# Retention values centred by a TensorE product, their copy on ScalarE, and the NSA compression one tile later

## The chip, the cores and the metric
One NeuronCore of one Trainium2 chip runs the whole program in one launch. The time is the device time of that core in microseconds: the median of three runs, with their lowest and highest. Every run computes two layers of the model below for a sequence of 512 positions.

## What is computed
Two layers of a mixer with four branches and a gated feed-forward part, all in float32. What matters here:

```python
h = rms_norm(x, norm1_g); z = h @ w_in            # 512 x 1024 times 1024 x D_IN
# retention, for each of 4 heads of 128: zq, zk, zv, zg from z
scores = einsum(q, k) * intra                     # decay mask
o = scores @ v (+ the state from earlier chunks)
mu  = mean(o, axis=-1); var = mean((o - mu)**2)
o = (o - mu) * rsqrt(var + EPS) * gn_g * silu(zg)
# NSA branch, compression of keys and values
tb  = t[:, blk] + cmp_pe                          # windows of 32, stride 16
hid = gelu(einsum('bnlgd,lde->bnge', tb, w1)); out = hid @ w2
k_c = rotary(compress(k_cmp)); v_c = compress(v_cmp)
```

The kernel does not subtract the mean of `o`: it centres each row of `v` over the 128 features of its head beforehand, which gives the same, since `o` is linear in `v`.

## The kernel before
All activations lie transposed, features on the 128 partitions and the 512 positions along the free axis. TensorE does every projection as 24 matmuls of 128x512: each float32 weight and each float32 activation is split into a high half and a low half in the type fp32r, and three products (high by high, high by low, low by high; L1185 to L1187) are added up in one PSUM bank, for eight chunks of 128 features. Such a product of one 128-column group of weights is called a tile here. The two banks `acc[0]` and `acc[1]` alternate; VectorE empties one (`take`, L717, multiplying by the norm's factor `rstd`) while TensorE fills the other, and `acc_free` counts the tiles emptied.

The weights stream through three slots: SP's queue loads a group of 512 KB, ScalarE makes its high half `w_hi` (`ahead`, L455, for the group two ahead, as soon as TensorE has finished the group before the present one), GpSimd makes the low half `w_lo` in two operations (L433), both with semaphores `hi_ready` and `lo_ready`. These are the only operations of GpSimd. ScalarE runs its program in order, so `ahead` stands behind whatever was written ahead of it.

A layer has four stages: 12 tiles of group A (keys, values, queries, gates; the list `A_TILES`), 32 tiles of group B (retention, short convolution, pool; `B_TILES`) beside which the attention runs, then a loop that merges the branches, then output and feed-forward. The order of group A is written out by hand on each engine: on TensorE a loop over `A_TILES` with extra steps after tile 5 (`compress`, L1268: 64 small products of the windows `win_k`, `win_v` with `w1k`, `w1v`), after tile 7 (`kc` and `vc`, from `hid`) and after tile 9 (`kc_swap`), and the turns of `v_slc` and `v_win` (L1277) after tiles 5 and 7; on VectorE a straight list (L811 to L853). The windows are made by L775 in four operations each. VectorE's `rotate` (L757, L759, L761) works on keys and queries with partners that ScalarE's DMA queue has copied into `rot`.

Group B has 128 slots, four to a tile, one after each quarter of the tile's 24 matmuls. The table `SIDE` lists for each slot what is done there, and every engine walks through it and does its own part. For head h of the retention, whose tiles rq, rk, rv, rg stand at `RET0[h]` = 0, 16, 20, 24, `ret_turn` is in the last slot of tile rg (15, 79, 95, 111). `ret_scores` and `ret_values` (L1408, L1418, with VectorE's L944 between them, which multiplies by the decay mask and makes `pr`) begin at `RET_SLOT[h]` = 68, 80, 96, 112. So for heads 1 to 3 the turn is in the slot just before the first scores, and for head 0 it is far ahead. `ret_end` of heads 0 to 3 (L973, L975) stands in slots 79, 88, 104 and 122: that of head 0 in the slot of head 1's turn, ahead of it. Its reciprocals are L964 and L967.

`ret_turn` before: TensorE turns the four 128x128 blocks of `rv_T` into one PSUM bank (`turn4`, L1277); VectorE sums each row of each block (L951, to `v_sum`) and writes `rv` as the block less 1/128 of that sum (L952). `ret_values` of the head waits for it through `t_free`. The banks `t_bank` are also used by the attention's turns until slot 70; `t_free` counts their release in the order of `T_USES`.

The last stage spreads the final norm's factors over the partitions by four products with the identity (L1523). Before the first tile TensorE multiplies zeros ten times (L1180).

Of the kernel before, what the change touches and what calls it, by code (L numbers as in the profile page):

```python
# [147 lines left out]
V_MADE = ["win_k", "k0_scaled", "k1_scaled", "win_v", "k0", "k1", "arg", "hid", "q0", "q1", "q2", "q3", "kc"]  # L148
# [13 lines left out]
V_MADE.append("branches")  # L162
# [20 lines left out]
def build(nc, xT, weights, vec, w1, pool_w, consts, decay, out):  # L183
    with ExitStack() as ctx:
# [72 lines left out]
        w2v = at("w2v", [P, DH], F32, R4 + 4 * QT * 3 * HEADS + 4 * 224)  # L257
        den = small[:, 64:68]
# [185 lines left out]
        def _(act):  # L444
# [64 lines left out]
            with act.Fori(0, LAYERS) as L:  # L509

                for g in range(A_GROUPS):
                    if g:
                        ahead(L, g)
                    if g == 3:
                        root("sumsq1", L)
                    if 1 <= g <= 4:
                        act.wait_ge(acc_free, 1 + L * TILES + g)
                        nc.scalar.activation((k_cmp[:, :], v_cmp[:, :], kT[:, 0, :], kT[:, 1, :])[g - 1], acc[(g - 1) % 2][:, :],
                                             ACT.Copy).then_inc(acc_free, 1)
                    for name in ("k0", "k1", "q0", "q1", "q2", "q3"):  # L520
                        if A_AT[name] == g - 1:
                            rotate_partners(L, name)
                    if g == 6:
                        act.wait_ge(v_made, v_count(L, "arg"))
                        nc.scalar.activation(hid_a, hid_a, ACT.Tanh, scale=0.7978845608028654).then_inc(a_made, 1)
                    if g == 11:
                        act.wait_ge(acc_free, 1 + L * TILES + 12)
                        nc.scalar.activation(sc[:, 2, :], sc[:, 2, :], ACT.Tanh, scale=0.5).then_inc(a_made, 1)


                for b in range(B_GROUPS):
# [15 lines left out]
                    for n in range(4 * b, 4 * b + 4):  # L547
                        for e in SIDE[n]:
# [14 lines left out]
                            elif e[0] == "attn_hi":  # L563
# [3 lines left out]
                                                     ACT.Copy).then_inc(a_made, 1)  # L567
                            elif e[0] == "ret_hi":
# [76 lines left out]
        def _(dve):  # L645
# [64 lines left out]
            with dve.Fori(0, LAYERS) as L:  # L710
# [111 lines left out]
                gelu_arg()  # L822
                t_wait("v_slc")
                t_end(ve.tensor_copy(v_nat[:, 0, :, :], t_of("v_slc")[:, :].rearrange("p (k n) -> p k n", k=QT)), "v_slc")
                gelu()
                take(6, qT[:, 0, :])
                take(7, qT[:, 1, :])
# [3 lines left out]

                s_wait("kc")
# [9 lines left out]
                take(8, qT[:, 2, :])  # L842
                rotate("q1", qT[:, 1, :], "cos_a", "sin_a")
# [7 lines left out]
                v_end(ve.tensor_tensor(kc[:, 0:NCMP], kc[:, 0:NCMP], kc_rot[:, 0:NCMP], ALU.add), "kc")  # L851
                dve.wait_ge(halves, 1 + L * (2 * GROUPS) + 24)
# [93 lines left out]
                def ret_turn(e):  # L946


                    t_wait(e)
                    src = t_of(e)[:, :].rearrange("p (k n) -> p k n", k=QT)  # L950
                    then(ve.tensor_reduce(v_sum, src, AX.X, ALU.add))  # L951
                    t_end(ve.scalar_tensor_tensor(out=rv[:, :, :], in0=v_sum.unsqueeze(2).to_broadcast([P, QT, RD]),  # L952
                                                  scalar=-1.0 / RD, in1=src, op0=ALU.mult, op1=ALU.add), e)
# [15 lines left out]
                def ret_end(e):  # L969
# [5 lines left out]
                    v_end(ve.scalar_tensor_tensor(out=o, in0=o, scalar=0.5, in1=rg[:, :], op0=ALU.mult, op1=ALU.mult), e)  # L975
# [198 lines left out]
        def _(pe):  # L1174
# [4 lines left out]
            for _ in range(10):  # L1179
# [9 lines left out]
            with pe.Fori(0, LAYERS) as L:  # L1189
# [91 lines left out]
                for g, name in enumerate(A_TILES):  # L1281
# [9 lines left out]
                    if g == 5:  # L1291
                        compress()
                    if g == 7:
# [104 lines left out]
                def ret_turn(e):  # L1398
                    pe.wait_ge(acc_free, 1 + L * TILES + (A_GROUPS + B_TILES.index(("rv", e[1])) + 2))
                    turn4(e, rv_T[:, :])  # L1400
# [121 lines left out]
            for t in range(QT):  # L1522
                ins = mm(s_bank[1][:, t * P:(t + 1) * P], spread(rstd[:, t:t + 1], [[0, P]]), ident, start=True, stop=True)  # L1523
# [4 lines left out]
CHAIN_LAYER, CHAIN_J, CHAIN_F, CHAIN_D = 179, 4, 15, 2  # L1528
# [117 lines left out]
```

## Time and profile before

| | |
|---|---|
| median of 3 runs | 2092.7 us (2092.09 to 2094.68) |
| profiled execution, its own time | 2092.94 us |
| its span, first to last instruction | 2091.2 us |
| mean granted TensorE clock | 0.992 of full |
| TensorE busy | 2044.3 us of the span |
| VectorE, ScalarE, GpSimd busy | 58%, 33%, 44% of the span |
| largest groups on TensorE | L1185 to L1187, the projections: 771.2, 743.3 and 744.0 us for `xg` alone |

The profiled execution is one more run of the same program; its time is 1.7 us more than its span, which runs from the first to the last instruction. "Busy" is the time in which an engine had an instruction under way. The matmuls overlap, the start of one lying before the end of the last, so the time of a group is read from starts rather than from durations. What ended an idle stretch of an engine is named behind "<-". A float32 product that is not a turn leaves two matmul records, so the x counts of such lines are twice the matmuls.

### The profile page before, as it was taken

To read this page: it belongs to the slowest core of one execution; us is meant where nothing else is said; L and a number is where in the kernel's file an instruction comes from. 1 tells how busy PE (TensorE), PEld (TensorE's weight loads), DVE (VectorE), ACT (ScalarE), POOL (GpSimd) and SP (SyncE) were. 2 spreads that over 40 slices of the span, in tenths; PEclk is the share of its full clock that TensorE was granted. 3 is DMA by queue.
4 is the path that set the end of the run, shared out by engine and by line. 5 is a ranking of instruction groups with operands and counts; after the bars stand their busy time and mean duration, and the time that the engine had idled before them with its cause. 6 is when DMAs were issued, how large, how long until landed. Compare 5 with 4: busy or idle time off the path is not lost.

```text
span 2091.2 us, 31895 instructions
## 1 busy us (share of the span) xinstructions
PE 2044.3 (98%) x9764; PEld 1637.6 (78%) x9764; DVE 1216.9 (58%) x1811; ACT 682.9 (33%) x1001; POOL 917.6 (44%) x672
## 2 busy tenths in 40 slices
PE   8999999999999999999999999899999999999997
PEld 6777667888888888888877777678888888888886
DVE  7766866523226888862257677663322278888522
ACT  5255523333232322222233554232323232222222
POOL 3422223444444555545544212335444455555552
PEclk9999999999999999999999999999999999999998
DMA  5311122223222222223233112222222222232333
GB/s 208 96 62 52 62 74 93 81 100 100 93 98 99 93 97 93 100 85 119 91 120 101 51 52 65 88 86 91 98 97 96 100 91 92 99 100 92 102 107 104
DMA packets 57431, 194.88 MB, mean 93 GB/s; under 512 B 7040, under 2 KB 7552, under 8 KB 57216
## 3 DMA queue, kind: packets, MB, share of 16 engines
q1 hardware_dynamic: 52576, 186.17, 26.6%
q10 hardware_dynamic: 4768, 7.61, 1.4%
q8 instruction: 48, 0.79, 0.2%
q14 instruction: 39, 0.32, 0.1%
HBM read 186.67 MB, written 2.10 MB: 90 GB/s over the span
## 4 chain that ended last, share of the span: by engine, by line
PE 87%; DVE 8%; issue 3%; ACT 1%; ACTq 0%; DMA 0%; DVEq 0%; SPq 0%
PE acc L1185 27%; PE acc L1187 26%; PE acc L1186 26%; PE o L1385 2%; PE s L1359 2%; PE t L1367 1%; PE o L1418 1%; PE s L1408 1%; DVE pT L967 1%; DVE pT L964 1%; DVE win_k L775 0%; DVE rk L759 0%; PE s L1268 0%; DMA w_raw<-weights_dram 0%; DVE rstd L748 0%
## 5 line engine op out<-in xcount | busy, mean ns | idle before, releaser
L433 POOL TENSOR_TENSOR w_lo<-w_raw,w_hi 128x512 fp32r<-128x512 f32 x668 | 917.4, 1394 | 1148.5 <-ACT w_hi L455 1132.3
L1185 PE MATMUL acc<-xg_hi,w_hi 128*128 128x512 f32 x1904 | 771.2, 405 | 5.6 <-DVE xg_lo L697 3.0
L1187 PE MATMUL acc<-xg_hi,w_lo 128*128 128x512 f32 x1904 | 744.0, 391 | 0.0
L1186 PE MATMUL acc<-xg_lo,w_hi 128*128 128x512 f32 x1904 | 743.3, 390 | 0.0
L455 ACT ACTIVATE w_hi<-w_raw 128x1024 fp32r<-128x1024 f32 x336 | 355.3, 1057 | 822.9 <-PE acc L1187 777.7
L1185 PEld LDWEIGHTS acc<-xg_hi,w_hi 128*128 128x128 f32 x1904 | 358.4, 188 | 114.9 <-issue 29.0
L1186 PEld LDWEIGHTS acc<-xg_lo,w_hi 128*128 128x128 f32 x1904 | 358.8, 188 | 77.8 <-issue 7.3
L1187 PEld LDWEIGHTS acc<-xg_hi,w_lo 128*128 128x128 f32 x1904 | 358.4, 188 | 76.7
L1062 DVE TENSOR_TENSOR work<-acc,rstd 128x512 f32<-128x512 f32 x64 | 44.1, 689 | 256.2 <-PE acc L1187 256.2
L1186 PE MATMUL acc<-act_lo,w_hi 128*128 128x512 f32 x352 | 136.9, 389 | 0.0
L1185 PE MATMUL acc<-act_hi,w_hi 128*128 128x512 f32 x352 | 136.9, 389 | 0.0
L1187 PE MATMUL acc<-act_hi,w_lo 128*128 128x512 f32 x352 | 136.9, 389 | 0.0
L1156 DVE SCALAR_TENSOR_TENSOR x<-acc,x 128x512 f32 x16 | 11.1, 693 | 159.9 <-PE acc L1187 159.9
L1068 DVE SCALAR_TENSOR_TENSOR work<-work,acc 128x512 f32<-128x512 f32 x64 | 44.0, 687 | 103.2 <-PE acc L1187 103.2
L1185 PE MATMUL acc<-y_hi,w_hi 128*128 128x512 f32 x256 | 99.6, 389 | 0.0
L1186 PE MATMUL acc<-y_lo,w_hi 128*128 128x512 f32 x256 | 99.6, 389 | 0.0
L1187 PE MATMUL acc<-y_hi,w_lo 128*128 128x512 f32 x256 | 99.6, 389 | 0.0
L620 ACT ACTIVATE work<-work 128x512 f32<-128x512 f32 x44 | 27.8, 632 | 189.3 <-DVE work L1111 189.3
L919 DVE COPY pT<-t 128x128 f32<-128x128 f32 (+3 forms) x128 | 56.6, 483 | 54.8 <-PE o L1385 54.7
L1187 PEld LDWEIGHTS acc<-act_hi,w_lo 128*128 128x128 f32 x352 | 66.1, 188 | 13.8
L1186 PEld LDWEIGHTS acc<-act_lo,w_hi 128*128 128x128 f32 x352 | 66.1, 188 | 13.7
L1185 PEld LDWEIGHTS acc<-act_hi,w_hi 128*128 128x128 f32 x352 | 66.1, 188 | 13.6
(207 smaller groups left out, 2237.4 us busy)
## 6 DMA issues: line engine op xcount, KB each, us to landing
w_raw<-weights_dram SPq DMA_DIRECT2D x339, 512.0 KB, 3.3
x<-xT_dram SPq DMA_DIRECT2D x8, 256.0 KB, 6.4
rot<-rq ACTq DMA_DIRECT2D x16, 128.0 KB
rot<-rk ACTq DMA_DIRECT2D x16, 128.0 KB
dec<-decay_dram ACTq DMA_DIRECT2D x8, 256.0 KB, 3.2
out_dram<-x SPq DMA_DIRECT2D x8, 256.0 KB, 2.7
con<-consts_dram SPq DMA_DIRECT2D x1, 1406.0 KB, 11.1
w1k<-w_dram SPq DMA_DIRECT2D x2, 512.0 KB, 8.8
```

The source lines that it names most:

```text
L433: nc.gpsimd.tensor_tensor(w_lo[:, slot, part], w_raw[:, slot, part], w_hi[:, slot, part].bitcast(F32), ALU.subtract).then_inc(lo_ready, 1)
L455: nc.scalar.activation(w_hi[:, slot, :], w_raw[:, slot, :], ACT.Copy).then_inc(hi_ready, 1)
L620: nc.scalar.activation(work[:, 2, :], work[:, 1, :], ACT.Tanh, scale=0.5).then_inc(silu_ready, 1)
L919: t_end(ve.tensor_copy(pT[:, u % 2, 0:w], t_of(e)[:, 0:w]), e)
L964: then(ve.reciprocal(pT[:, 1, 0:S // 2], pT[:, 1, 0:S // 2]))
L1062: ve.tensor_tensor(work[:, n, :], acc[n % 2][:, :], rstd[:, :], ALU.mult).then_inc(acc_free, 1)
L1068: ve.scalar_tensor_tensor(out=work[:, n, :], in0=work[:, n, :], scalar=1.0, in1=acc[n % 2][:, :], op0=ALU.add, op1=ALU.mult).then_inc(acc_ ...
L1185: mm(tile, w_h, right_hi, start=first, stop=False)
L1186: mm(tile, w_h, right_lo, start=False, stop=False)
L1187: return mm(tile, w_l, right_hi, start=False, stop=last)
L1359: mm(b[:, 0:w], qT[r, h % 4, qi * P:(qi + 1) * P], kT[r, br, 0:w], start=True, stop=True).then_inc(s_done, 1)
L1385: ins = mm(o_bank[qi % 2][d, j * P:(j + 1) * P], v[:, d], p[:, half, :], start=(br == 0 and k == 0), stop=(br == 1 and k == qi + 1))
```

## The change
- `ret_turn` on TensorE is four matmuls of the blocks of `rv_T` with the matrix `center` = identity - 1/128, in place of four turns, so the centred values come out of PSUM ready. VectorE's sum and subtraction go; for head 0 VectorE copies the bank to `rv`, for heads 1 to 3 ScalarE does, in its walk through `SIDE`, and counts `t_free`.
- `center` (128x128, float32) is made on VectorE once a layer, as the last thing after `kc`.
- `compress` on TensorE moves from after tile 5 to after tile 6, the products of `hid` from after tile 7 to after tile 8. On VectorE `gelu_arg` moves behind take(6), `gelu` behind take(7), and the evictions of `kc` and `vc` behind take(8) and the rotation of `q1`. On ScalarE the tanh of `hid` moves from step 6 to step 7, behind the DMAs for `q0`.
- `ret_end` waits for its own last operation.
- The zero products at the start are 14 instead of 10, and the four products of the last stage become turns.

```diff
-V_MADE = [..., "q3", "kc"]
+V_MADE = [..., "q3", "kc", "center"]
...
+        center = at("center", [P, P], F32, R4 + 4 * QT * 3 * HEADS + 4 * 224 + 4 * DH)
...
 (ScalarE, group A)
-                    if g == 6:
+                    if g == 7:
                         act.wait_ge(v_made, v_count(L, "arg"))
                         nc.scalar.activation(hid_a, hid_a, ACT.Tanh, ...)
 (ScalarE, SIDE)
+                            elif e[0] == "ret_turn" and e[1]:
+                                act.wait_ge(t_done, t_use(L, e))
+                                nc.scalar.activation(rv[:, :, :], t_of(e)[:, :].rearrange("p (k n) -> p k n", k=QT), ACT.Copy).then_inc(t_free, 1)
...
 (VectorE, group A)
                 take(5, sc[:, 1, :])
-                gelu_arg()
                 t_wait("v_slc")
                 t_end(ve.tensor_copy(v_nat[:, 0, :, :], ...), "v_slc")
+                take(6, qT[:, 0, :])
+                gelu_arg()
+                take(7, qT[:, 1, :])
                 gelu()
-                take(6, qT[:, 0, :])
-                take(7, qT[:, 1, :])
                 t_wait("v_win")
                 t_end(ve.tensor_copy(v_nat[:, 1, :, :], ...), "v_win")
                 rotate("q0", qT[:, 0, :], "cos_a", "sin_a")
+                take(8, qT[:, 2, :])
+                rotate("q1", qT[:, 1, :], "cos_a", "sin_a")
                 s_wait("kc")
                 ...
                 s_end(ins, "vc")
-                take(8, qT[:, 2, :])
-                rotate("q1", qT[:, 1, :], "cos_a", "sin_a")
                 take(9, qT[:, 3, :])
...
                 v_end(ve.tensor_tensor(kc[:, 0:NCMP], kc[:, 0:NCMP], kc_rot[:, 0:NCMP], ALU.add), "kc")
+                v_end(ve.scalar_tensor_tensor(out=center[:, :], in0=ones, scalar=-1.0 / RD, in1=ident, op0=ALU.mult, op1=ALU.add), "center")
...
 (VectorE, SIDE)
                 def ret_turn(e):
+                    if e[1]:
+                        made["t"] += 1
+                        return
                     t_wait(e)
-                    src = t_of(e)[:, :].rearrange("p (k n) -> p k n", k=QT)
-                    then(ve.tensor_reduce(v_sum, src, AX.X, ALU.add))
-                    t_end(ve.scalar_tensor_tensor(out=rv[:, :, :], in0=v_sum.unsqueeze(2).to_broadcast([P, QT, RD]),
-                                                  scalar=-1.0 / RD, in1=src, op0=ALU.mult, op1=ALU.add), e)
+                    t_end(ve.tensor_copy(rv[:, :, :], t_of(e)[:, :].rearrange("p (k n) -> p k n", k=QT)), e)
...
-                    v_end(ve.scalar_tensor_tensor(out=o, in0=o, scalar=0.5, in1=rg[:, :], ...), e)
+                    v_end(ve.scalar_tensor_tensor(out=o, in0=o, scalar=0.5, in1=rg[:, :], ...), e, wait=True)
...
 (TensorE)
-            for _ in range(10):
+            for _ in range(14):
                 mm(acc[1][:, 0:P], rstd[:, 0:P], rstd[:, 0:P], start=True, stop=True)
...
-                    if g == 5:
+                    if g == 6:
                         compress()
-                    if g == 7:
+                    if g == 8:
                         pe.wait_ge(v_made, v_count(L, "hid"))
...
                 def ret_turn(e):
                     pe.wait_ge(acc_free, ...)
-                    turn4(e, rv_T[:, :])
+                    if e[1] == 0:
+                        pe.wait_ge(v_made, v_count(L, "center"))
+                    b = t_begin(e)
+                    last_wait()
+                    for k in range(QT):
+                        ins = mm(b[:, k * P:(k + 1) * P], rv_T[:, k * P:(k + 1) * P], center[:, :], start=True, stop=True)
+                    ins.then_inc(t_done, 1)
...
             for t in range(QT):
-                ins = mm(s_bank[1][:, t * P:(t + 1) * P], spread(rstd[:, t:t + 1], [[0, P]]), ident, start=True, stop=True)
+                ins = nc.tensor.transpose(s_bank[1][:, t * P:(t + 1) * P], spread(rstd[:, t:t + 1], [[0, P]]), ident)
...
-CHAIN_LAYER, CHAIN_J, CHAIN_F, CHAIN_D = 179, 4, 15, 2
+CHAIN_LAYER, CHAIN_J, CHAIN_F, CHAIN_D = 175, 4, 15, 2
```

## Rows read from the trace of the kernel before

**Rows 1.** The page's busy times: busy us (share of the span) xinstructions.
```profile
PE 2044.3 (98%) x9764; PEld 1637.6 (78%) x9764; DVE 1216.9 (58%) x1811; ACT 682.9 (33%) x1001; POOL 917.6 (44%) x672
```

**Rows 2.** TensorE's waits: line waited for: us in total, times, longest.
```profile
PE o L1418 <- DVE pr L944: 12.6, 8, 3.9
PE s L1268 <- DVE win_v L775: 7.0, 2, 3.5
...
PE s L1408 <- DVE rk L761: 3.4, 4, 1.4
```

**Rows 3.** TensorE's timeline, tiles 5 to 7 of layer 0: start, duration, what.
```profile
49.09 0.28 PE L1268 MATMUL s<-win_k,w1k 128*64 128x62 f32 x1 [3.49 <-DVE win_v L775]
...
52.88 0.94 PE L1277 MATMUL t<-con,sc 128*128 128x128 f32 x4
53.58 0.47 PE L1185 MATMUL acc<-xg_hi,w_hi 128*128 128x512 f32 x1
...
59.15 0.39 PE L1185 MATMUL acc<-xg_hi,w_hi 128*128 128x512 f32 x1
```

**Rows 4.** Timelines of ScalarE, GpSimd and TensorE, head 1, layer 0.
```profile
281.75 1.06 ACT L455 ACTIVATE w_hi<-w_raw 128x1024 fp32r<-128x1024 f32 x1 [4.21 <-PE acc L1187]
...
282.89 2.99 POOL L433 TENSOR_TENSOR w_lo<-w_raw,w_hi 128x512 fp32r<-128x512 f32 x2 [2.74 <-ACT w_hi L455]
...
289.66 2.05 PE L1418 MATMUL o<-pr,rv 128*128 128x512 f32 x2 [3.88 <-DVE pr L944]
```

**Rows 5.** Busy time by window: PE, PEld, DVE, ACT, POOL, granted clock, DMA, GB/s.
```profile
289.66:300.10 10.44, 10.44 (x30) 7.22 (x31) 2.47 (x5) 1.06 (x1) 0.70 (x1) 0.70 0.01 2
1322.31:1331.38 9.07, 9.07 (x30) 6.57 (x31) 2.47 (x5) 1.06 (x1) 0.69 (x1) 0.81 0.01 2
```

**Rows 6.** Timelines of VectorE and TensorE, head 2, layer 0.
```profile
318.48 1.78 DVE L761 TENSOR_TENSOR rk<-rk,rot 128x512 f32<-128x512 f32 x1
...
320.49 1.10 PE L1408 MATMUL s<-rq,rk 128*128 128x512 f32 x2 [1.41 <-DVE rk L761]
...
323.50 1.10 PE L1418 MATMUL o<-pr,rv 128*128 128x512 f32 x2 [0.52 <-DVE pr L944]
```

**Rows 7.** TensorE's timeline, head 3, layer 0.
```profile
353.26 1.10 PE L1418 MATMUL o<-pr,rv 128*128 128x512 f32 x2 [0.50 <-DVE pr L944]
```

**Rows 8.** VectorE's timeline, take(4) and the last add before take(5), layer 0.
```profile
45.00 0.69 DVE L717 TENSOR_TENSOR sc<-acc,rstd 128x512 f32<-128x512 f32 x1
...
54.43 0.69 DVE L761 TENSOR_TENSOR kT<-kT,rot 128x512 f32<-128x512 f32 x1
```

**Rows 9.** VectorE's `kc` and TensorE's product of the compressed keys, layer 0.
```profile
87.32 1.26 DVE L851 TENSOR_TENSOR kc<-kc,kc_rot 128x31 f32<-128x31 f32 x1
...
89.61 1.09 PE L1339 MATMUL s<-qT,kc 64*32 64x512 f32 x16
```

**Rows 10.** TensorE's timeline: the zero products at the start; the turns of head 2.
```profile
1.71 4.40 PE L1180 MATMUL acc<-rstd 128*128 128x128 f32 x20 [1.71 <-DVE rstd L683]
...
317.10 0.60 PE L1277 MATMUL t<-con,rv_T 128*128 128x128 f32 x4
```

**Rows 11.** VectorE, head 1, layer 0; last, durations of L973 over all heads, min/median/max.
```profile
282.97 1.77 DVE L973 SCALAR_TENSOR_TENSOR pT<-pT,vec 128x512 f32<-128x512 f32 x1
284.77 1.67 DVE L975 SCALAR_TENSOR_TENSOR pT<-pT,rg 128x512 f32<-128x512 f32 x1
286.36 0.68 DVE L951 TENSOR_REDUCE small<-t 128x4 f32<-128x512 f32 x1
...
L973 DVE SCALAR_TENSOR_TENSOR pT<-pT,vec x8: 750/753/1767, 283.0 to 1403.6; 128x512 f32<-128x512 f32 x8
```

**Rows 12.** TensorE's timeline, the end of the program.
```profile
2078.06 1.87 PE L1519 MATMUL s<-con,ssq 128*128 128x1 f32 x8 [2.41 <-DVE ssq L1084]
2080.50 2.08 PE L1523 MATMUL s<-con,rstd 128*128 128x128 f32 x8 [0.57 <-DVE rstd L1166]
```

**Rows 13.** TensorE's timeline, the first matmul of tile 2, layer 0.
```profile
22.69 0.47 PE L1185 MATMUL acc<-xg_hi,w_hi 128*128 128x512 f32 x1 [0.80 <-ACT k_cmp L518]
```

More of the change, by code:

```diff
@@ L146 @@
 assert len(S_USES) % 2 == 0 and len(T_USES) % 2 == 0
-V_MADE = ["win_k", "k0_scaled", "k1_scaled", "win_v", "k0", "k1", "arg", "hid", "q0", "q1", "q2", "q3", "kc"]
+V_MADE = ["win_k", "k0_scaled", "k1_scaled", "win_v", "k0", "k1", "arg", "hid", "q0", "q1", "q2", "q3", "kc", "center"]
 A_MADE = ["hid", "gate"]
@@ L161 @@
             V_MADE.append(_e[1])
-V_MADE.append("branches")
+V_MADE += ["branches"]
 PV_MADE = [_x for _e in SEQUENCE for _x in ([_e, ("values", _e[1] + 1)] if _e[0] == "values" else [_e] if _e[0] == "ret_values" else [])]
@@ L974, in ret_end @@
                                                  op0=ALU.mult, op1=ALU.mult))
-                    v_end(ve.scalar_tensor_tensor(out=o, in0=o, scalar=0.5, in1=rg[:, :], op0=ALU.mult, op1=ALU.mult), e)
+                    v_end(ve.scalar_tensor_tensor(out=o, in0=o, scalar=0.5, in1=rg[:, :], op0=ALU.mult, op1=ALU.mult), e, wait=True)
                 def ret_split(e):
```

## The prediction
> **What bounds the kernel now.** The busy times first: TensorE is busy 98% of the span [rows 1], so only TensorE's instructions and its idle time count. The list of its waits comes next: three of them belong to stages that this diff touches, 7.0, 12.6 and 3.4 us in both layers together [rows 2]. The timelines then show the place of each. (a) After tile 5 it stands 3.49 us for VectorE's `win_v` before compressing [rows 3], and again in layer 1 [rows 2]. (b) In head 1 of the retention it stands 3.88 us for `pr` and then runs at a granted clock below full: 0.70 over 10.44 us, 0.81 over 9.07 us in layer 1 [rows 4, 5]; 0.5 of full is the lower of its two levels (1.2 of 2.4 GHz). (c) Heads 2 and 3 show waits of 1.41, 0.52 and 0.50 us [rows 6, 7]; the totals [rows 2] leave about 0.3 for the fourth (3.4 / 2 - 1.41). The sum is made against the profiled execution, 2092.94 us; the median of the runs is 0.24 us less.
>
> **Compression one tile back.** TensorE leaves tile 5 at 49.09 - 3.49 = 45.6. The turn of `v_slc` waits for take(4), done at 45.69 [rows 8], costs about 0.4, so tile 6 starts at 46.2 and lasts 59.15 - 53.58 = 5.57 [rows 3]: 51.8. The compression takes 52.88 - 49.09 = 3.8 [rows 3]: 55.6. Tile 7 also needs its accumulator emptied by take(5), behind the rotation of `k1`. Its last add starts at 54.43 and takes 0.69 [rows 8], the take another 0.6: 55.8 at best. But ScalarE's next high half starts when tile 6 ends, now 51.8, so GpSimd's next low half (from 53.8, when its present one is through, to 56.4) falls on that add, and an add between SBUF tiles beside GpSimd takes 1.78 instead of 0.69 [rows 6]. I take 56.8, a new wait of 1.2. Tile 7 started at 59.15, so 2.35 us are gained, 2.3 in layer 1: **-4.65**. Bounds: -6.6 without that collision, -2.6 if a second operation collides. `hid` moves with tiles 7 and 8 and has a tile (5.6 us) of time. `kc` now comes after the rotation of `q1`, some 5 us into tile 9 (take 0.69, three operations of 0.69, 1.78 and 1.78, `kc` itself 0.2 [rows 6, 8]), whose end asks for it at 6.1 us (5.57 and the small products): no wait, slack 1.1. ScalarE's DMAs for the rotations keep their order and follow the takes; its tanh stands behind the four for `q0` instead of before them, ready 5 us before it is needed. SP's and GpSimd's queues are passed by nothing.
>
> **`center`.** One VectorE operation of 128 columns a layer, behind `kc`. Free it would take some 0.3 us. The operation before it has 31 columns and takes 1.26 us [rows 9], which only waiting for GpSimd explains; GpSimd then has one more half to do. So I take 1.3 us, until 89.9; the gate copy behind it must free its bank (0.3 us more, with the hand-over 90.4) before L1339, now at 89.61 [rows 9]. **+1.5** for two layers; bounds 0 (it slips in) and +2.6.
>
> **Product in place of turn.** A turn of four blocks is four records, 0.60 us with the drain of the last [rows 10]. A plain product leaves two records (L1408 is one matmul, "x2" [rows 6]). At the low level 20 records took 4.40 us, 0.22 each [rows 10], so about 0.11 at full clock. Four more records of 0.11 to 0.13 make +0.5 us a head. In head 0 nothing covers it: **+1.0** for two layers. In head 1 it falls into the wait. Bounds a head: 0.44, and 1.35 if a plain product cost four turns (3 x 0.45; rival 3). The Trainium skill, "TensorE: Matmul & The Clock Gate", Terms, speaks against the change here: it calls transpose mode 4x faster for FP32. The two records of L1408 say a factor of two, and the sum goes by them; by the page it would be rival 3's 2081.6. Head 0's VectorE work falls from 1.3 to 0.7 us, worth nothing: it lies beside 16 units of attention in which TensorE is the bound.
>
> **Head 1.** The chain to `pr` on VectorE is L973, L975, L951, L952, take, L944 [rows 11]. L951 goes, 0.68 us, and L952, 128x512 like it: 1.3 us. The added wait at the end of `ret_end` costs about 0.1 (L975, which needs L973, starts 0.03 after its end; L951, which doesn't need L975, 0.08 before its end [rows 11]). And L973 and L975 take 1.77 and 1.67 where the median of L973 is 0.75 [rows 11], since GpSimd's halves start at 282.89, right behind ScalarE's w_hi of 281.75 to 282.81 [rows 4]. The diff puts ScalarE's copy of `rv` ahead of that w_hi: it waits for the products (now turns, over just before that w_hi; done near 282.6), copies (0.6: w_hi takes 1.06 for twice the columns), so w_hi starts near 283.2 and GpSimd near 284.3, when L973 and L975 are through (283.0 + 0.75 + 0.69 = 284.4). That is another 2.0 us. L1418 starts 3.2 us earlier, at 286.45; TensorE, 0.5 later than before, is there at 286.3. **-6.4** for two layers. Bounds: -2.4 if GpSimd still collides, -6.7 if TensorE's arrival is the limit. The weights lose nothing: w_hi and w_lo of a tile two ahead start 1.4 us later with over 5 us to spare.
>
> **The clock behind it.** Lost now: 0.30 x 10.44 = 3.1 and 0.19 x 9.07 = 1.7 us [rows 5]. With 0.2 us of idle in place of 3.88 no fall is left: **-4.8**. Idle stretches of 1.41 and less [rows 6] show no fall; one of 2.41 us at the end does: L1523 takes 0.24 us a record there [rows 12]. Bounds: 0, -4.8.
>
> **Heads 2 and 3.** In head 2 L761 runs into GpSimd (1.78) [rows 6]; with ScalarE's w_hi delayed again it takes 0.69, and `rk` is ready 1.1 us earlier. TensorE comes 0.5 us later by the products, so of 1.41 + 0.52 some 1.4 is gained: **-2.8**. Head 3: 0.32 + 0.50 - 0.5 = 0.3: **-0.6**. Bounds of the two: -0.2 and -4.2.
>
> **Ends.** Four products become turns at the tail: four records of 0.24 less [rows 12]: **-0.95**. Four more warming products (8 records, at most 1.8 us) end before the first real one at 9.1 (1.71 + 4.40 + 1.8 = 7.9). If they kept the clock up, tile 0 would end earlier, but tile 2 waits 0.80 us for ScalarE's `k_cmp`, behind its own queue [rows 13]: 0. Bounds -0.5, +0.3.
>
> Sum: -4.65 + 1.5 + 1.0 - 6.4 - 4.8 - 2.8 - 0.6 - 0.95 = **-17.7**, so 2092.94 - 17.7 = 2075.2; that is 2075.0 against the median, which I leave at 2075.2.
>
> **Rivals.**
> (1) GpSimd still collides: ScalarE's w_hi is not held back enough, or L973 starts late. Head 1 gains only 2.4; its idle time of 3.88 - 1.2 - 0.5 = 2.2 is nearest to the 2.41 that had the clock fall, so nothing of 4.8; heads 2 and 3 give 1.4. Sum -4.65 + 1.5 + 1.0 - 2.4 - 1.4 - 0.95 = -6.9: 2086.0. For it: the margin is 0.1 to 0.2 us. Against: a held operation only collides if it starts after GpSimd's. Chance 0.17.
> (2) The small collisions do not come: the compression gives 6.6 and `center` costs nothing: 2092.94 - 17.7 - 1.95 - 1.5 = 2071.8. Chance 0.15.
> (3) A plain product costs four turns, 1.35 us more a head: head 0 +2.7, head 1 -5.0, clock -4.8, head 2 -1.2, head 3 +1.1. With -4.65, +1.5 and -0.95: -11.3, 2081.6. The two records of L1408 speak against it. Chance 0.05.
> (4) The change does not do what it says: the copy of `rv` on ScalarE comes as late as VectorE's did, and the waits of heads 1 to 3 stay, clock and all. Left: -4.65 + 1.5 + 1.0 - 0.95 = -3.1, 2089.8. It needs ScalarE busy over 5 us at 282; it has one w_hi there. Chance 0.05.
> (5) Slower: `kc` late. TensorE stands at `kc_swap` behind tile 9, with all later products queued behind it, if `kc` comes more than 1.1 us later than worked out. To end over 4.2 us slower, the wait with its clock loss would have to be (17.7 + 4.2) / 2 = 11 us a layer; with a whole rotation (4.2) and a clock loss like head 1's (3.1) added to rival 1 it gives 2086.0 + 14.6 = 2100.6. Chance 0.02.
>
> **Numbers.** Forecast 0.56, the rivals 0.44. The likeliest case alone spans 2072.5 to 2078.5. The range 2071.0 to 2086.5 holds it, rivals 2 and 3 and over half of rival 1; some 0.17 is outside. A measurement of this kernel can tell 0.2% (4.2 us) from no change. Faster than 2088.5: 0.92 (forecast, rivals 2, 3, nearly all of 1); within: 0.06 (4, the rest of 1); slower: 0.02.
>
> **What would show it.** L1268 without its 3.5 us waits, a new wait of about 1.2 us for L717 at tile 7; a `center` operation of 1.3 us (0.3 would be rival 2) and L1339 0.7 us late; eight records to a head's product in 0.9 us (1.8: rival 3); L973 and L975 at 0.75 and 0.69 in head 1, L1418 waiting under 0.5 us there; a granted clock of 1.00 through the retention. If L973 or L975 stays at 1.7, rival 1; if the idle time at L1418 stays at 3.9, rival 4; a wait at L1313 for `kc`, rival 5.

## The result, and the profile after

The changed kernel takes **2073.1 us** (median of 4 runs, 2072.6 to 2073.9) against 2093.1 us of the kernel before, run beside it (4 runs, 2092.1 to 2094.7): a ratio of 0.9904, with an interval of 0.9887 to 0.9921. The profiled execution took 2072.95 us, its span 2071.1, so traces can be compared with medians here. The forecast was 2075.2: the sign and the size hold, and the result lies 2.1 us below it, inside the range.

Line numbers after are higher by 1 to 10: the projections are L1189 to L1191 (before L1185 to L1187), the takes L721, the last add of a rotation L765, `ret_end` L977 and L979, the decay mask L949, the scores L1418, the values L1428, the new products L1409, the copy of `rv` on ScalarE L571.

The busy times of the page, against [rows 1]: TensorE's work is 1.1 us less in a span 20 us shorter. What went is idle time and slow time.

```profile
PE 2043.2 (99%) x9800; PEld 1637.2 (79%) x9800; DVE 1209.7 (58%) x1799; ACT 685.6 (33%) x1007; POOL 917.5 (44%) x672
```

TensorE's waits, against [rows 2] (what waits <- what it waits for: us in total, times, longest):

```profile
PE acc L1189 <- DVE sc L721: 3.6, 4, 1.3
PE o L1428 <- DVE pr L949: 2.4, 2, 1.2
...
PE acc L1189 <- ACT k_cmp L519: 1.6, 1, 1.6
```

The wait of `compress` for `win_v` (7.0 us) is gone, so is that of the scores for `rk` (3.4), and the wait for `pr` has fallen from 12.6 to 2.4 us; what is left of it is head 0's, once a layer. New is a wait for a take, 1.3 us at tile 7.

**Compression.** TensorE's and VectorE's timelines from tile 5 to tile 7, layer 0:

```profile
45.33 0.63 PE L1281 MATMUL t<-con,sc 128*128 128x128 f32 x4 [0.34 <-DVE sc L721]
...
56.51 0.47 PE L1189 MATMUL acc<-xg_hi,w_hi 128*128 128x512 f32 x1 [1.27 <-DVE sc L721]
```
```profile
52.31 1.76 DVE L763 TENSOR_TENSOR kT<-kT,con 128x512 f32<-128x512 f32 x1
54.11 1.65 DVE L765 TENSOR_TENSOR kT<-kT,rot 128x512 f32<-128x512 f32 x1
55.68 0.68 DVE L721 TENSOR_TENSOR sc<-acc,rstd 128x512 f32<-128x512 f32 x1
```

Tile 7 starts at 56.51 where it started at 59.15 [rows 3]. The add that took 0.69 us before [rows 8] takes 1.65 now, since GpSimd's halves run from 50.56 to 56.89 over it:

```profile
50.56 6.33 POOL L434 TENSOR_TENSOR w_lo<-w_raw,w_hi 128x512 fp32r<-128x512 f32 x4 [6.85 <-ACT w_hi L456]
```

**`center`.** Timelines of VectorE behind `kc`, of GpSimd and of TensorE's keys, against [rows 9]. `center` took 0.28 us, and TensorE's product has no wait behind it.

```profile
84.83 1.26 DVE L855 TENSOR_TENSOR kc<-kc,kc_rot 128x31 f32<-128x31 f32 x1
86.02 0.28 DVE L856 SCALAR_TENSOR_TENSOR center<-con 128x128 f32<-128x128 f32 x1
```
```profile
86.01 1.44 POOL L434 TENSOR_TENSOR w_lo<-w_raw,w_hi 128x512 fp32r<-128x512 f32 x1
```
```profile
87.15 1.09 PE L1343 MATMUL s<-qT,kc 64*32 64x512 f32 x16
```

GpSimd's next half is recorded from 86.01 on, 0.01 us ahead of `center`, and it took 1.44 us. In experiment 6 it went the other way once.

**Head 1.** Timelines of ScalarE, GpSimd, VectorE and TensorE, against [rows 4, 11]:

```profile
280.51 0.60 ACT L571 ACTIVATE rv<-t 128x512 f32<-128x512 f32 x1 [5.20 <-PE t L1409]
281.01 1.05 ACT L456 ACTIVATE w_hi<-w_raw 128x1024 fp32r<-128x1024 f32 x1
```
```profile
282.13 2.53 POOL L434 TENSOR_TENSOR w_lo<-w_raw,w_hi 128x512 fp32r<-128x512 f32 x2 [4.21 <-ACT w_hi L456]
```
```profile
277.89 0.69 DVE L721 TENSOR_TENSOR rv_T<-acc,rstd 128x512 f32<-128x512 f32 x1
...
280.55 0.75 DVE L977 SCALAR_TENSOR_TENSOR pT<-pT,vec 128x512 f32<-128x512 f32 x1
281.33 0.69 DVE L979 SCALAR_TENSOR_TENSOR pT<-pT,rg 128x512 f32<-128x512 f32 x1
```
```profile
279.42 1.05 PE L1409 MATMUL t<-center,rv_T 128*128 128x128 f32 x8
...
284.14 1.10 PE L1428 MATMUL o<-pr,rv 128*128 128x512 f32 x2
```

ScalarE's copy stands ahead of w_hi, GpSimd starts at 282.13, behind both operations of `ret_end` (L977 and L979, over at 282.02), which take 0.75 and 0.69 instead of 1.77 and 1.67. The values follow the products of the head by 4.72 us, where they followed the turns by 8.11 (281.55 to 289.66), and no wait stands there. The windows of ten us behind it, against [rows 5] (columns as there):

```profile
284.14:294.14 10.00, 10.00 (x41) 7.38 (x42) 2.47 (x5) 2.46 (x4) 3.07 (x3) 1.00 0.27 79
1306.77:1316.77 10.00, 10.00 (x41) 7.37 (x42) 2.47 (x5) 2.44 (x4) 3.02 (x3) 1.00 0.29 80
```

The clock stays full. In heads 2 and 3 no wait for `rk` or `pr` is left, against [rows 6, 7].

**The ends.** The last stage's products as turns, against 2.08 us for the products [rows 12]; and the start, where tile 2 still waits for ScalarE [rows 13]:

```profile
2061.45 1.12 PE L1533 MATMUL s<-con,rstd 128*128 128x128 f32 x4 [0.57 <-DVE rstd L1170]
```
```profile
22.06 0.47 PE L1189 MATMUL acc<-xg_hi,w_hi 128*128 128x512 f32 x1 [1.57 <-ACT k_cmp L519]
```

**Where the 20.0 us of the span came from** (2091.16 to 2071.14). Each row is the growth of the lead that one instruction's start has over its start before, from the one named to the next, in both layers (us):

| stretch | forecast | layer 0 | layer 1 |
|---|---|---|---|
| start, to tile 2 | 0 | 0.63 | |
| compression, to tile 7 | 2.35 + 2.3 | 2.01 | 2.19 |
| tile 7 to the keys (`center`) | -0.75 each | -0.18 | -0.20 |
| head 0's products | -0.5 each | -0.53 | -0.44 |
| head 0's values | 0 | 0.22 | 0.22 |
| head 1, products to values | 3.2 each | 3.39 | 3.32 |
| behind it (the clock), to head 2's products | 3.1 + 1.7 | 2.84 | 1.45 |
| head 2 | 1.4 each | 1.66 | 1.67 |
| head 3 | 0.3 each | 0.58 | 0.55 |
| tail | 0.95 | | 1.09 |

The layers' columns add up to 20.5; between the stretches some 0.4 us is lost again in small pieces. The 0.63 of the start is no work of the change: x reached ScalarE 0.67 us earlier in that execution (its first operation on it at 6.88, before 7.55), and tile 2's start differs between the executions shown below by 1.45 us (21.82 to 23.27).

In layer 0 of the kernel before, the clock fell behind the compression's wait as well. Windows (columns as in [rows 5]) of that kernel, and of experiment 1's in the same place, where a wait of 3.48 us was followed by no fall:

```profile
50.10:53.51 3.41, 3.41 (x53) 3.28 (x50) 3.26 (x3) 2.00 (x2) 2.62 (x2) 0.50 0.04 10
```
```profile
49.00:53.00 4.00, 3.88 (x65) 3.73 (x66) 3.84 (x5) 2.34 (x2) 2.08 (x2) 1.00 0.07 14
```

It cost little: from the compression's start to `v_win`'s turn it is 16.18 us with that fall (49.09 to 65.27) and 15.90 without (49.12 to 65.02). So 0.3 of the 2.01 us is clock; in layer 1 the same stretch is 15.92 us in spite of a fall, and nothing of the 2.19 is.

### The profile page after: what moved, and what is told of

Same layout as the page of the kernel before. It is cut to its first block, busy times and chain, and to the rows that moved or that the text cites. A ratio compares the mean times of both kernels' runs of the same rounds, so it can differ in the third digit from the quotient of the medians.

```text
span 2071.1 us, 31913 instructions
## 1 busy us (share of the span) xinstructions
PE 2043.2 (99%) x9800; PEld 1637.2 (79%) x9800; DVE 1209.7 (58%) x1799; ACT 685.6 (33%) x1007; POOL 917.5 (44%) x672
## 4 chain that ended last, share of the span: by engine, by line
PE 93%; DVE 4%; issue 1%; ACT 1%; DMA 0%; ACTq 0%; SPq 0%; DVEq 0%
PE acc L1189 28%; PE acc L1191 28%; PE acc L1190 28%; PE o L1389 2%; PE s L1363 2%; PE t L1371 1%; PE o L1428 1%; PE s L1418 1%; PE t L1409 0%; DVE win_k L779 0%; DMA w_raw<-weights_dram 0%; PE s L1444 0%; PE s L1435 0%; DVE rstd L752 0%; DVE sc L721 0%
## 5 line engine op out<-in xcount | busy, mean ns | idle before, releaser
L1189 PE MATMUL acc<-xg_hi,w_hi 128*128 128x512 f32 x1904 | 769.5, 404 | 6.5 <-DVE sc L721 3.6
L1191 PE MATMUL acc<-xg_hi,w_lo 128*128 128x512 f32 x1904 | 742.9, 390 | 0.0
L1189 PEld LDWEIGHTS acc<-xg_hi,w_hi 128*128 128x128 f32 x1904 | 357.4, 188 | 116.5 <-issue 33.4
L1191 PEld LDWEIGHTS acc<-xg_hi,w_lo 128*128 128x128 f32 x1904 | 357.3, 188 | 76.4
L1189 PE MATMUL acc<-act_hi,w_hi 128*128 128x512 f32 x352 | 136.9, 389 | 0.0
L1191 PE MATMUL acc<-act_hi,w_lo 128*128 128x512 f32 x352 | 136.9, 389 | 0.0
L1189 PE MATMUL acc<-y_hi,w_hi 128*128 128x512 f32 x256 | 99.6, 389 | 0.0
L1191 PE MATMUL acc<-y_hi,w_lo 128*128 128x512 f32 x256 | 99.6, 389 | 0.0
L1191 PEld LDWEIGHTS acc<-act_hi,w_lo 128*128 128x128 f32 x352 | 66.1, 188 | 13.8
L1189 PEld LDWEIGHTS acc<-act_hi,w_hi 128*128 128x128 f32 x352 | 66.1, 188 | 13.7
```

The lines of the kernel that those rows point to most:

```text
L1189: mm(tile, w_h, right_hi, start=first, stop=False)
L1191: return mm(tile, w_l, right_hi, start=False, stop=last)
```

## The experiments

**1. Only the order of ScalarE against VectorE.** The kernel before, with its turns and VectorE's centring; ScalarE waits before the next w_hi.

```diff
+ elif e[0] == "ret_turn" and e[1]:        # ScalarE's walk through SIDE
+     act.wait_ge(v_made, v_count(L, ("ret_end", 0) if e[1] == 1 else ("rk", e[1])))
```

> The kernel before, with one wait added on ScalarE: in the slot of the turns of heads 1 to 3 it does not start the next w_hi until VectorE's ret_end of head 0 (head 1) or the rotation of rk (heads 2, 3) is over, so GpSimd's low half can't start beside them. Nothing is removed. Theory (two of the three us of head 1 come from GpSimd's collisions): L973 and L975 fall to 0.75 and 0.69 in head 1, TensorE's wait at L1418 from 3.88 to about 1.9, L1408's in head 2 from 1.41 to 0.3 to 0.5; with 1.9 us of idle the clock may or may not fall, so 2093 - (4 + 2 + 0 to 4.8) = 2082 to 2087. Rival (only the two VectorE operations that the change removes count): unchanged within 1 us, or slower, because the weights come later: 2092 to 2096.

Measured: 2084.4 us median (2081.6 to 2085.8, 5 runs), ratio 0.9963 (0.9948 to 0.9977). In the profiled execution (2081.64, the fastest of the five) the timelines of VectorE and TensorE show `ret_end` undisturbed, and the values of head 1 waiting half as long:

```profile
282.70 0.75 DVE L975 SCALAR_TENSOR_TENSOR pT<-pT,vec 128x512 f32<-128x512 f32 x1
283.48 0.69 DVE L977 SCALAR_TENSOR_TENSOR pT<-pT,rg 128x512 f32<-128x512 f32 x1
```
```profile
287.40 1.10 PE L1420 MATMUL o<-pr,rv 128*128 128x512 f32 x2 [1.87 <-DVE pr L946]
```

From the turns to the values it is 6.10 us (281.30 to 287.40) instead of 8.11: 2.0 us, the collision's price as forecast. From there to head 2's turns it is 24.49 us in this kernel and 27.44 in the kernel before: 2.95 us of clock, 1.57 in layer 1. Head 2's wait for `rk` falls from 1.41 to 0.30 us. One wait a head on ScalarE, which computes nothing different, brings most of what head 1 was to give.

The other four runs were not traced. Their spans are 1.9 to 4.1 us longer, and three of them record a mean granted clock of 0.993 or 0.994, against 0.996 in the traced one (the fourth has 0.944, which its span doesn't bear out). The traced executions in which the clock fell behind head 1 have 0.992 to 0.995. So it is not known whether the clock stayed up behind a wait of 1.87 us in those four.

**2. The copy behind w_hi.** The changed kernel, with ScalarE's copy of `rv` one place later.

```diff
  ahead(L, A_GROUPS + b)
+ for h in range(1, RH):
+     if b == RET0[h] + 4:  ... the wait for t_done and the copy of rv ...
  ...
- elif e[0] == "ret_turn" and e[1]:  ...
```

> The changed kernel with ScalarE's copy of rv behind the next w_hi instead of ahead of it; same work. Theory: GpSimd's low half starts at its old place again, L977 and L979 of head 1 take 1.7 to 1.8 again, pr comes 2.0 us later, TensorE waits about 2 us at L1428 of head 1 in each layer and 0 to 0.5 us for rk in head 2; no or a partial clock fall: 2073 + 4 to 9 = 2077 to 2082. Rival (order on ScalarE does not matter): 2073 within 1 us.

Measured: 2078.5 us (2077.6 to 2079.8, 4 runs), ratio 0.9934 (0.9917 to 0.9950): 5.4 us slower than the changed kernel by the medians. VectorE's timeline in heads 1 and 2:

```profile
280.10 0.74 DVE L979 SCALAR_TENSOR_TENSOR pT<-pT,vec 128x512 f32<-128x512 f32 x1
280.88 1.65 DVE L981 SCALAR_TENSOR_TENSOR pT<-pT,rg 128x512 f32<-128x512 f32 x1
...
310.73 1.67 DVE L767 TENSOR_TENSOR rk<-rk,rot 128x512 f32<-128x512 f32 x1
```

The collisions are back in each head, and with them waits of 0.91 us in head 1 and 0.84 and 0.82 for `rk` in heads 2 and 3; products to values take 0.87 to 1.00 us longer in each of the three. So it isn't only that the copy went to another engine; where it stands on ScalarE counts. Its place counts for more than its length: w_hi starts 0.19 us behind TensorE's first product here and 1.59 in the changed kernel, since the copy of 0.60 us first waits for the products. But in head 1 one operation collides, not two, and the next run shows the same.

**3. The copy on VectorE in all heads.**

```diff
- elif e[0] == "ret_turn" and e[1]:  ...        # ScalarE
- if e[1]:
-     made["t"] += 1
-     return                                    # VectorE copies all
```

> The changed kernel with the copy of rv on VectorE in all four heads; ScalarE has no part. The product still stands in place of the turn. Theory: VectorE's chain in head 1 is 0.6 us shorter than before the change instead of 3.2 (collisions back, one operation instead of two), so TensorE waits 3.9 - 0.6 - 0.5 = 2.8 us there, the clock falls in both layers (2 to 5 us together), head 2 waits for rk as before: 2073 + 5.2 + 3.4 + 2 = about 2083, range 2080 to 2086. Rival (the product alone brings the gain, wherever the copy is made): 2073 to 2076.

Measured: 2079.4 us (2078.7 to 2079.9, 4 runs), ratio 0.9936 (0.9919 to 0.9952). That is a miss by some 4 us, and the head shows it: 1.51 us of waiting and no fall of the clock.

```profile
280.76 0.74 DVE L971 SCALAR_TENSOR_TENSOR pT<-pT,vec 128x512 f32<-128x512 f32 x1
281.53 1.65 DVE L973 SCALAR_TENSOR_TENSOR pT<-pT,rg 128x512 f32<-128x512 f32 x1
```
```profile
281.04 3.30 POOL L434 TENSOR_TENSOR w_lo<-w_raw,w_hi 128x512 fp32r<-128x512 f32 x2 [2.83 <-ACT w_hi L456]
```
```profile
285.90 1.10 PE L1422 MATMUL o<-pr,rv 128*128 128x512 f32 x2 [1.51 <-DVE pr L946]
```

GpSimd starts 0.28 us after the first operation of `ret_end` here; before it started 0.08 us ahead of it (282.89 and 282.97 [rows 4, 11]). VectorE takes `rv_T` 1.62 us ahead of TensorE's products here and 1.53 in the changed kernel, against 1.24 us before the turns in the kernel before (280.31 and 281.55), so it comes 0.3 us earlier against TensorE. The operation that had started was not slowed: 0.74 us, not 1.77. 0.3 us earlier is worth 1.0 us. Why VectorE is earlier was not found; ScalarE's DMAs for `rk` go out 0.35 us earlier against head 0's values.

**4. The compression alone.** The kernel before with the moves of the third item of the change, on all three engines, and nothing else.

> The kernel before with only the compression moved one tile back (with its order on VectorE and ScalarE). Theory: the waits of 3.49 us at L1268 go, a new wait of 0.9 to 1.3 us at tile 7 comes, 2.2 us a layer gained: 2093 - 4.2 = about 2089. Rival (the move only shifts the wait, since the same VectorE chain follows): 2092 to 2094. Second rival (the clock fall that follows the wait now costs more than the wait): 2086 or less.

Measured: 2088.8 us (2086.3 to 2092.4, 10 runs), ratio 0.9984 (0.9974 to 0.9993); profiled 2088.48. TensorE's timeline, tiles 5 to 7:

```profile
46.06 0.63 PE L1277 MATMUL t<-con,sc 128*128 128x128 f32 x4 [0.34 <-DVE sc L717]
52.10 0.30 PE L1268 MATMUL s<-win_k,w1k 128*64 128x62 f32 x1
...
56.97 0.47 PE L1185 MATMUL acc<-xg_hi,w_hi 128*128 128x512 f32 x1 [1.00 <-DVE sc L717]
```

This is what was expected (2089). The wait of 3.49 us became 0.34 + 1.00, 2.2 us less a layer. Head 1's wait stays as it was (3.86 at 287.75, 3.89 in layer 1): the two parts of the change don't touch each other. The windows of ten us behind it:

```profile
287.75:297.75 10.00, 10.00 (x35) 7.07 (x36) 2.47 (x5) 1.06 (x1) 1.53 (x2) 0.83 0.01 2
1316.89:1326.89 10.00, 10.00 (x31) 7.00 (x32) 2.47 (x5) 1.06 (x1) 0.76 (x1) 0.74 0.01 2
```

Here the longer fall is in layer 1 (6.8 us at the lower level, 3.4 in layer 0); in the kernel before it was in layer 0. The four waits differ by 0.03 us at most.

**5. What the products cost.** The changed kernel with turns where its products are. The mean of the values is not subtracted in this kernel.

```diff
- ins = mm(b[:, k * P:(k + 1) * P], rv_T[:, k * P:(k + 1) * P], center[:, :], start=True, stop=True)
+ ins = nc.tensor.transpose(b[:, k * P:(k + 1) * P], rv_T[:, k * P:(k + 1) * P], ident)
```

> The changed kernel with the four products of each head put back to four turns with the identity (the mean of the values is not subtracted: the centring is left out); the copies stay where they are. It prices a product against a turn. Theory (eight records against four, about 0.47 us a head, and nothing hidden any more since no wait is left in heads 2 and 3): 4 x 2 x 0.47 = 3.8, less what VectorE's chain holds back in head 1: 2073.1 - 2.5 to 3.8 = 2069.3 to 2070.6. Rival (a plain product costs four turns, 1.35 us more a head): 2062 to 2064.

Measured: 2072.6 us (2070.8 to 2074.4, 4 runs), ratio 0.9906 (0.9890 to 0.9923), not to be told from the changed kernel, where 2069.3 to 2070.6 was expected; profiled 2070.83, 2.1 less, of which 1.05 is head 0's (below) and 0.24 an earlier start of tile 2 (21.82). TensorE's waits in this kernel name what covers the price in heads 1 to 3:

```profile
PE o L1428 <- DVE pr L949: 3.3, 4, 1.2
...
PE s L1418 <- DVE rk L765: 1.8, 4, 0.6
```

Without the products' extra 0.5 us TensorE waits 0.42 us for `pr` in head 1, 0.55 and 0.34 for `rk` in heads 2 and 3. So the expectation missed what covers it. The price is paid in head 0 alone: from its products to its scores it is 140.49 us in the changed kernel and 139.93 here, 0.56, and 0.49 in layer 1. Four turns' time for a product (rival 3) would have shown some 1.35 us there.

**6. Both ends undone.**

```diff
-            for _ in range(14):
+            for _ in range(10):
...
-  ins = nc.tensor.transpose(s_bank[1][:, t * P:(t + 1) * P], spread(rstd[:, t:t + 1], [[0, P]]), ident)
+  ins = mm(s_bank[1][:, t * P:(t + 1) * P], spread(rstd[:, t:t + 1], [[0, P]]), ident, start=True, stop=True)
```

> The changed kernel with both ends as before: ten zero products instead of 14, four products in place of the four turns in the last stage. Theory: the first tile runs slower (its first matmuls 0.4 us apart instead of 0.23), but tile 2 waits for ScalarE's k_cmp either way, so the start gives 0; the end gives back 0.95 us: 2074.0. Rival (the zero products brought the 0.6 us by which tile 2 started earlier in the changed kernel): 2074.7, with tile 2 starting at 22.7 instead of 22.1.

Measured: 2073.7 us (2073.3 to 2077.8, 4 runs), ratio 0.9915 (0.9898 to 0.9931): as expected, though 0.6 us is less than these runs can tell. The trace says more of the start and of the tail:

```profile
8.91 0.80 PE L1189 MATMUL acc<-xg_hi,w_hi 128*128 128x512 f32 x1 [2.57 <-DVE xg_lo L701]
9.50 0.63 PE L1190 MATMUL acc<-xg_lo,w_hi 128*128 128x512 f32 x1
...
2061.62 1.26 PE L1533 MATMUL s<-con,rstd 128*128 128x128 f32 x8 [0.96 <-DVE rstd L1170]
```

With ten zero products the first tile runs slowly from 9.50 on (0.63 us an instruction, 0.43 apart); with fourteen it ran 0.23 apart. Tile 2's wait for `k_cmp` is gone in exchange, and the compression starts 0.41 us later than in the changed kernel, where x had arrived 0.47 us earlier (7.35 and 6.88). The four products more gain nothing, as forecast. The tail's products ran at full clock in this execution, 1.26 us for the eight records; the clock fell at 2062.54, just behind the last one's start. The turns' 1.12 us in the changed kernel were at the lower level, so these two don't price the change. Experiment 3 has turns whose first 0.19 us were at full clock:

```profile
2068.32 0.96 PE L1527 MATMUL s<-con,rstd 128*128 128x128 f32 x4 [0.96 <-DVE rstd L1164]
```

So the turns save 1.0 us only where the clock has fallen, and at full clock 0.3 us or somewhat more; no trace has them wholly at full clock.

In layer 0 of this execution `center` did what the prediction had said of it. VectorE's and TensorE's timelines:

```profile
86.21 1.42 DVE L856 SCALAR_TENSOR_TENSOR center<-con 128x128 f32<-128x128 f32 x1
```
```profile
88.01 1.09 PE L1343 MATMUL s<-qT,kc 64*32 64x512 f32 x16 [0.61 <-DVE gates L864]
```

GpSimd's half, recorded from 86.20 on, took 1.27 us and `center` 1.42. From tile 7 to the keys it is 31.36 us (56.65 to 88.01) against 30.64 in the changed kernel: 0.72 us. Over the six kernels that have `center`, in both layers, it took 0.28 us eleven times and 1.42 once.

**7. A version that may be better.** The changed kernel, with the take that tile 7 waits for ahead of the rotation that held it up.

```diff
+                take(5, sc[:, 1, :])
                 rotate("k1", kT[:, 1, :], "cos_a", "sin_a")
-                take(5, sc[:, 1, :])
```

> The changed kernel with VectorE's take(5) moved ahead of the rotation of k1, so that the accumulator of tile 7 is free before TensorE asks for it. Theory: the new waits of 1.27 and 0.85 us at tile 7 go, nothing else moves: 2073.1 - 2.1 = 2071.0. Rival (the rotation of k1, now 0.6 us later, makes v_slc, take(6) or the arguments of the gelu late, and the wait turns up at tile 8): 2073 within 0.5.

Measured: 2071.9 us (2071.5 to 2071.9, 4 runs), ratio 0.9899 (0.9883 to 0.9916); profiled 2071.91. VectorE at tile 6:

```profile
50.79 0.69 DVE L765 TENSOR_TENSOR kT<-kT,rot 128x512 f32<-128x512 f32 x1
51.40 0.68 DVE L721 TENSOR_TENSOR sc<-acc,rstd 128x512 f32<-128x512 f32 x1
52.12 1.22 DVE L761 TENSOR_TENSOR rot<-rot,con 128x512 f32<-128x512 f32 x1
```

From the compression's start to `v_win`'s turn it is 9.40 us (52.59 to 61.99) instead of 10.67, and 9.39 instead of 10.29 in layer 1: 1.27 and 0.90, the waits of 1.27 and 0.85. That x arrived late in this execution (tile 2 at 23.27, 1.21 us behind) hides half of it in the span. The expectation was 2071.0. The intervals of this version and of the changed kernel overlap.

**8 and 9. How long must TensorE stand for its clock to fall?** Experiment 1's kernel, with one and with two reductions more on VectorE in head 1.

```diff
- then(ve.tensor_reduce(v_sum, src, AX.X, ALU.add))
+ for _ in range(2 if e[1] == 1 else 1):          # 3 in the second kernel
+     then(ve.tensor_reduce(v_sum, src, AX.X, ALU.add))
```

> The kernel before with ScalarE held back as in the first experiment, and in head 1 VectorE sums the values once more than needed (one more reduction of 128x512, some 0.7 us, ahead of the subtraction). TensorE's wait for pr in head 1 should be 1.87 + 0.71 = 2.6 us. Theory that only a wait near the 3.9 us of the kernel before makes the clock fall: no fall, so the time of the first experiment, 2081.6 in its profiled execution, and 1.4 us for two layers: 2083.0. Rival, the row that the prediction leaned on (a fall follows idle time of 2.4 us, as at the end of the program): 3.1 and 1.7 us more, 2087.8, with a granted clock below 0.9 in the ten us behind head 1.

> As the kernel with one more reduction, but with two more: a wait of 1.87 + 1.42 = 3.3 us in head 1. If the clock stays up: 2081.6 + 2.8 = 2084.4. If it falls as in the kernel before: 2084.4 + 4.8 = 2089.2, with a granted clock of 0.7 to 0.8 in the ten us behind head 1.

Measured: 2087.0 us (2085.3 to 2089.3, 10 runs), ratio 0.9974 (0.9964 to 0.9983), profiled 2086.75; and 2088.8 us (2083.8 to 2091.5, 10 runs), ratio 0.9979 (0.9970 to 0.9989), profiled 2088.85. TensorE's values of head 1, with one more reduction, and the windows behind them in both layers:

```profile
288.69 1.10 PE L1421 MATMUL o<-pr,rv 128*128 128x512 f32 x2 [2.59 <-DVE pr L946]
```

```profile
288.69:298.69 10.00, 10.00 (x35) 7.40 (x36) 2.47 (x5) 1.06 (x1) 1.62 (x2) 0.83 0.17 54
1317.76:1327.76 10.00, 10.00 (x36) 7.20 (x37) 2.47 (x5) 1.08 (x2) 1.84 (x2) 0.86 0.19 57
```

The windows behind head 1 of experiment 1's kernel, and of that with two more:

```profile
287.40:297.40 10.00, 10.00 (x41) 7.35 (x42) 2.47 (x5) 2.44 (x4) 3.10 (x3) 1.00 0.29 80
```
```profile
288.84:298.84 10.00, 10.00 (x36) 7.06 (x37) 2.47 (x5) 1.06 (x1) 1.67 (x2) 0.84 0.17 54
```

| traced execution of | wait in head 1 | values to head 2's turn or product, layers 0 and 1 |
|---|---|---|
| changed | 0 | 24.60, 24.62 |
| experiment 1 | 1.87 | 24.49, 24.50 |
| one more reduction | 2.59 | 26.10, 25.87 |
| two more | 3.32 | 26.04, 26.15 |
| compression alone | 3.86, 3.89 | 26.19, 26.93 |
| before | 3.88, 3.86 | 27.44, 26.07 |

My theory for the first of them falls: 2.59 us brings the fall already, as the row of the tail that the prediction leaned on had it. A fall cost 1.4 to 1.7 us in six of the eight cases of this table, and 2.4 and 2.95 in the two where it was the longer one. What makes a fall the longer one was not found: it came behind waits of 3.88 and 3.89 us, the shorter one behind 3.86 and 3.86 and all smaller ones. The next 0.7 us taken away, from 2.59 to 1.87, bring 1.6 and 1.4 us of clock in these traces.

That is one execution of each kernel, and the length of the wait alone doesn't decide. Experiment 1's other runs were named above. One of the ten runs with two more reductions took 2083.8 us at a mean granted clock of 0.996, about what was expected of it if the clock stays up (2084.4). And ahead of the compression 3.48 us brought no fall once.

## Why the prediction was right, and where it was not

- **What bounds, and the sum's make-up: right.** 13.6 of the 17.7 us were to come from the retention's heads and the clock behind them, 4.65 from the compression; the trace has 14.9 and 4.2 (table; head 0's values, which were not forecast, are 0.44 of the 14.9).
- **Compression: right, 0.45 too high.** The add collided with GpSimd as forecast (1.65 us for 1.78), the new wait is 1.27 (1.2 forecast), 0.85 in layer 1. Alone it gives 2.2 us a layer (experiment 4). The prediction put nothing for the clock here, though it fell behind this wait too; that was worth 0.3 us in layer 0. "Bounds: -6.6 without that collision" is near what experiment 7 reaches in another way: it takes the take out from behind the add.
- **`center`: wrong in this execution.** The step that failed is "The operation before it has 31 columns and takes 1.26 us [rows 9], which only waiting for GpSimd explains; GpSimd then has one more half to do. So I take 1.3 us". GpSimd did have one more half to do, but the two starts lie 0.01 us apart, and `center` took 0.28 us, its bound below. In layer 0 of experiment 6 the same pair went as forecast: 1.42 us, and the keys 0.72 us later for 0.75 forecast. So the mechanism exists and comes rarely (once in twelve); what was wrong is to count on it. The term is 0.4 at most (the table's 0.18 and 0.20, which have no wait behind them), not 1.5. With the heads' terms below and the start's 0.63, against which the compression and the clock gave a little less, that makes the 2.1 us: the total is as close as it is partly because misses of both signs cancel.
- **Product in place of turn: right.** 0.53 and 0.44 us in head 0 for 0.5. The price is two records for one, as [rows 6] had it, and not what the Trainium skill states in "TensorE: Matmul & The Clock Gate", Terms (transpose mode 4x faster for FP32): rival 3 is out by experiment 5, where the four products were turned back and head 0 gained 0.56 us. What covers it in heads 1 to 3 was named right, and shows as waits of 0.34 to 0.55 us once it is gone.
- **Head 1: right, by its mechanism too.** 3.39 and 3.32 us for 3.2. Experiment 1 has the collision's part alone, 2.0 us as forecast. The prediction counted its margin of 0.1 to 0.2 us to the end of `ret_end` (it was 0.11: over at 282.02, GpSimd from 282.13). By experiment 3 what counts is the start of its second operation, at 281.33: a margin of 0.80. What the prediction didn't see: VectorE comes 0.3 us earlier against TensorE in this head, so half of the collision would have gone even without the copy ahead of w_hi (experiments 2 and 3). Rival 1 was therefore too dear: with one of the two collisions back in head 1 and those of heads 2 and 3 the kernel takes 2078.5, not 2086.0.
- **Clock: right, 0.5 too high.** 2.84 and 1.45 us for 3.1 and 1.7. That the two layers were sized 3.1 and 1.7 comes from the one execution that was read; experiment 4's gives 1.7 and 2.4 for the same wait. Rival 1's assumption for a wait of 2.2 us stays open, between 1.87 (no fall in the traced execution) and 2.59 (a fall).
- **Heads 2 and 3: right in kind, 1.1 too low in sum.** 1.66, 1.67, 0.58 and 0.55 us for 1.4 and 0.3 each. All waits went (1.93 us in head 2 [rows 6]), as forecast. The term mis-sized is the 0.5 set against them. From its products to its values head 2 takes 4.74 us; with turns (experiment 5) it takes 4.88, of which 0.55 is the wait, so the products cost 0.4 there. And 6.40 us of before less its waits is 4.47, not 4.33: 0.14 more went with the waits than the trace lists as idle.
- **Head 0's values: not forecast,** 0.22 us a layer (a wait of 1.22 us instead of 1.44).
- **Ends: right.** 1.09 us for 0.95 at the tail, and nothing from the zero products. Experiment 6 adds that the tail's gain needs the low clock there, which the kernel before had in the execution that was read and does not always have.

Of the rivals, 2 ("The small collisions do not come", 2071.8) is half true: `center`'s did not, the compression's did.

## What to carry to other kernels

When two engines slow each other on one kind of operation, look at who starts first: moving a cheap operation on a third engine by one place can be worth more than taking work away, here 5.4 us over three heads of two layers for a copy of 0.6 us. A wait on TensorE has its own price and can have that of the clock behind it: 1.4 to 2.95 us in all eight traced cases of 2.59 us and more in head 1, nothing in the two of 1.87. One execution doesn't settle it, so look at the granted clock of all runs before a gain is put down to it. And before a tile's accumulator is waited for, look whether its take stands behind work that nobody waits for.

## What the runs showed of the hardware that was not expected

- Where an operation of VectorE between SBUF tiles and one of GpSimd's halves start within 0.02 us of each other, either can be the one that is slowed. `center`, 128x128, took 0.28 us and the half 1.44 in the changed kernel; it took 1.42 and the half 1.27 in layer 0 of experiment 6.
- Behind the tail's wait of 2.41 us the clock fell in all eleven traced executions, but not at the same time: from 0.45 us ahead of the wait's end (the kernel before, 2077.61 and 2078.06) to 2.93 us behind it (experiment 6, 2062.54 and 2059.61). So the eight records of the last products took 2.08 us in one and 1.26 in the other.
- Ahead of the first tile the clock fell, or was low already, in all six traced executions with ten zero products (idle time of 1.99 to 3.00 us, records 0.43 us apart) and in none of the five with fourteen (0.50 to 2.48 us).
- Behind head 1's wait a fall cost 1.4 to 1.7 us in six of eight cases and 2.4 and 2.95 in two, at granted clocks of 0.83 to 0.86, 0.74 and 0.69 over the ten us behind it.
